# A feed-forward's up projection: every second pair of weight units by seven quarter products

## The reference

```python
def conv_ffn(h, w_up, conv_w, conv_b, w_down):
    u = h @ w_up                                   # 512x1024 by 1024x5632
    ch = u.shape[-1]
    u = lax.conv_general_dilated(u, conv_w, window_strides=(1,), padding=((CONV_W - 1, 0),),
                                 dimension_numbers=('NWC', 'WIO', 'NWC'), feature_group_count=ch) + conv_b
    g, val = jnp.split(u, 2, axis=-1)
    return (jax.nn.gelu(g) * val) @ w_down
```

## Time and profile before

| | |
|---|---|
| three runs | 1375.34, 1376.65, 1377.49 us (median 1376.65) |
| the profiled execution | 1374.93 us, its span 1373.2 us |
| TensorE | 1351.9 us busy, 9440 matmuls |
| VectorE, ScalarE, GpSimd | 743.1, 670.6, 794.4 us busy |
| DMA | 122.81 MB, mean 89 GB/s |
| up projection, from unit 4 on | 435.2 to 652.8 us |

### The profile page before, as it was taken

The page is one execution under the profiler, slowest core; times in us unless marked ns, Lnnn a source line. Parts: engine busy times, 40 slices in busy tenths (PEclk is TensorE's granted clock), DMA queues, the critical chain, the costliest instruction groups (busy, mean ns, idle before and its releaser), DMA issues.

```text
span 1373.2 us, 24197 instructions
## 1 busy us (share of the span) xinstructions
PE 1351.9 (98%) x9440; PEld 1140.9 (83%) x9440; DVE 743.1 (54%) x995; ACT 670.6 (49%) x1172; POOL 794.4 (58%) x599
## 2 busy tenths in 40 slices
PE   9999999999999999999999999999999999999998
PEld 7888787778889888888888887788888878999987
DVE  5135456366556333333554857344379957777732
ACT  4245665364357444444322568566463434445543
POOL 7643342373266666566566447954268856656782
PEclk9999999999999999999999999999999999999999
DMA  6332221221040222222332312200023222233222
GB/s 226 127 119 77 77 77 46 93 106 62 32 169 32 99 101 92 94 105 92 107 107 95 121 50 90 76 19 4 3 79 137 92 93 92 99 102 107 96 104 77
DMA packets 34508, 122.81 MB, mean 89 GB/s; under 512 B 3824, under 2 KB 4336, under 8 KB 34288
## 3 DMA queue, kind: packets, MB, share of 16 engines
q1 hardware_dynamic: 33696, 119.31, 25.5%
q10 hardware_dynamic: 720, 2.20, 0.5%
HBM read 119.40 MB, written 2.10 MB: 88 GB/s over the span
## 4 chain that ended last, share of the span: by engine, by line
PE 91%; issue 3%; DVE 2%; POOL 2%; ACT 2%; ACTq 0%; POOLq 0%; DVEq 0%
PE ps L591 15%; PE ps L593 15%; PE ps L592 15%; PE ps L1427 3%; PE ps L1429 3%; PE ps L1428 3%; PE ps L1358 2%; PE ps L1360 2%; PE ps L1359 2%; PE ps L1495 1%; PE ps L1496 1%; PE ps L1497 1%; POOL w_lo L2231 1%; PE ps L722 1%; PE ps L709 1%
## 5 line engine op out<-in xcount | busy, mean ns | idle before, releaser
L2231 POOL TENSOR_TENSOR w_lo<-stage,w_hi 128x512 fp32r<-128x512 f32 x378 | 556.2, 1496 | 369.1 <-ACT w_hi L1526 364.6
L1526 ACT ACTIVATE w_hi<-stage 128x512 fp32r<-128x512 f32 x376 | 215.4, 623 | 103.2 <-DMA stage<-w 88.0
L591 PE MATMUL ps<-x_hi,w_lo 128*128 128x512 f32 x664 | 262.6, 395 | 0.0
L592 PE MATMUL ps<-x_lo,w_hi 128*128 128x512 f32 x664 | 258.6, 389 | 0.0
L593 PE MATMUL ps<-x_hi,w_hi 128*128 128x512 f32 x664 | 258.6, 389 | 0.0
L591 PEld LDWEIGHTS ps<-x_hi,w_lo 128*128 128x128 f32 x664 | 124.7, 188 | 29.1 <-issue 2.6
L592 PEld LDWEIGHTS ps<-x_lo,w_hi 128*128 128x128 f32 x664 | 124.7, 188 | 26.0 <-issue 1.0
L593 PEld LDWEIGHTS ps<-x_hi,w_hi 128*128 128x128 f32 x664 | 124.6, 188 | 26.1
L2415 POOL TENSOR_TENSOR w_lo<-stage,w_hi 128x512 fp32r<-128x512 f32 x44 | 75.4, 1744 | 53.9 <-DVE s_val L3135 53.9
L2769 DVE SCALAR_TENSOR_TENSOR conv<-ps,vcol,conv 128x511 f32<-128x511 f32 x44 | 33.0, 749 | 132.2 <-ACT conv L1741 132.0
L1741 ACT ACTIVATE conv<-ps,vcol 128x512 f32<-128x512 f32 x44 | 34.3, 779 | 121.1 <-PE ps L593 120.1
(11 more groups left out here) (515 smaller groups left out, 3322.4 us busy)
## 6 DMA issues: line engine op xcount, KB each, us to landing
stage<-w SPq DMA_DIRECT2D x210, 512.0 KB, 3.2
extra_stage<-w SPq DMA_DIRECT2D x6, 512.0 KB, 5.4
H<-xT SPq DMA_DIRECT2D x3, 512.0 KB, 8.6
mem<-memT SPq DMA_DIRECT2D x2, 512.0 KB, 10.6
pool_n<-pool_count ACTq DMA_DIRECT2D x1, 1024.0 KB, 6.1
outT<-outs SPq DMA_DIRECT2D x4, 256.0 KB, 2.0
outT<-outs SPq DMA_DIRECT2D x2, 384.0 KB, 2.7
stage<-w SPq DMA_DIRECT2D x2, 256.0 KB, 3.3
```

The lines of the kernel that those rows point to most:

```text
L591: pe.matmul(out, wl, hi(k), start=first, stop=False)
L592: pe.matmul(out, wh, lo(k), start=False, stop=False)
L1526: act.activation(unit_hi(b)[:, cols], unit_stage(b)[:, cols], ACT.Copy).then_inc(whi_made, 1)
L2231: pool.tensor_tensor(unit_lo(b)[:, cols], unit_stage(b)[:, cols], unit_hi(b)[:, cols].bitcast(F32), ALU.subtract).then_inc(wlo_made, 1)
```

## The change

Eight of the 22 pairs, p = 5, 7, ..., 19, are made by seven quarter products; the other pairs stay whole, in other banks than before where p is even and above 4. The results of a changed pair build up in the rows UX0, UX1, UY0, UY1 of 256 columns in banks 4 to 7, with UE for a product that both columns of the second row get. A running sum is copied by ScalarE from one row to the next (`up_copy`) and TensorE goes on adding on top of the copy; two products of the identity at the start of the stage open the two rows that are never started by a product. `up_add` adds UE at the end, and the taps read two neighbouring rows as one of 512. VectorE's queue gets the weight sums of pair p + 2 (`up_sums`), their low parts and, beside pairs 1 to 3, the four differences of the input. The loops of 12 units are written out. Two DMAs (levels, scan_keep) move from ScalarE's queue after the attention to the end of this stage, because the differences lie where they used to land. The branch stage only counts from other thresholds.

```diff
 UP_BANKS = 4
-UP_TURN = UP_BANKS * AHEAD
+UP_SEVENTHS = tuple(range(5, 20, 2))
...
+        UT_AT = ((24, 28), (80, 84), (A0 + 88, A0 + 92), (A0 + 40, A0 + 84))
+        ut_hi = [at(f"ut_hi{n}", [P, QB, HS], hi, F32R) for n, (hi, lo) in enumerate(UT_AT)]
+        ut_lo = [at(f"ut_lo{n}", [P, QB, HS], lo, F32R) for n, (hi, lo) in enumerate(UT_AT)]
+        ut_val = [at(f"ut_val{n}", [P, QB, HS], lo) for n, (hi, lo) in enumerate(UT_AT)]
+        US_AT = ((101.5, 103.5), (109.5, 111.5), (A0 + 96, 113.5))
+        us_hi = [at(f"us_hi{n}", [P, UNIT // 2], hi, F32R) for n, (hi, lo) in enumerate(US_AT)]
+        us_lo = [at(f"us_lo{n}", [P, UNIT // 2], lo, F32R) for n, (hi, lo) in enumerate(US_AT)]
+        us_val = [at(f"us_val{n}", [P, UNIT // 2], lo) for n, (hi, lo) in enumerate(US_AT)]
...
+        UX0, UX1, UY0, UY1, UE = 9, 10, 13, 14, 15
+        SEVENTHS = len(UP_SEVENTHS)
+        flat = ps[:].rearrange("p b n -> p (b n)")
+        def up_bank(t):
+            p = t // 2
+            return 2 * (p // 2 % 2) + t % 2 if p >= UP_SEVENTHS[0] and p % 2 == 0 else t % UP_BANKS
+        def up_row(t):
+            if t // 2 in UP_SEVENTHS:
+                first = (UX0, UY0)[t % 2] * HS
+                return flat[:, first:first + SEQ]
+            return ps[:, up_bank(t), :]
...
-            with pe.Fori(0, (2 * FFB - UP_BANKS) // UP_TURN) as i:
-                for t in range(UP_BANKS, UP_BANKS + UP_TURN):
-                    up_product(t, i)
-            for t in range(UP_BANKS + (2 * FFB - UP_BANKS) // UP_TURN * UP_TURN, 2 * FFB):
-                up_product(t)
+            def up_seventh(n, wh, wl, hi, lo, start=False):
+                out = quarter[:, n, :]
+                for k in range(QB):
+                    cols = slice(k * P, (k + 1) * P)
+                    pe.matmul(out, wl[:, cols], hi[:, k, :], start=start and k == 0, stop=False, skip_group_check=True)
+                    pe.matmul(out, wh[:, cols], lo[:, k, :], start=False, stop=False, skip_group_check=True)
+                    mm = pe.matmul(out, wh[:, cols], hi[:, k, :], start=False, stop=(k == QB - 1), skip_group_check=True)
+                return mm
+            def up_pair(p):
+                n, b = UP_SEVENTHS.index(p), U0["up"] + 2 * p
+                left, right = slice(0, UNIT // 2), slice(UNIT // 2, UNIT)
+                hi0, lo0, hi1, lo1 = (t[:, (b + d) % RING, :] for d in range(2) for t in (w_hi, w_lo))
+                B11, B21, B22 = ([t[:, QB * r:QB * r + QB, HALF[c]] for t in (x_hi, x_lo)] for r, c in ((0, 0), (1, 0), (1, 1)))
+                T1, T2, T3, T4 = ([ut_hi[j][:], ut_lo[j][:]] for j in range(4))
+                pe.wait_ge(ff_conv, UP_BANKS + 2 * p - 2)
+                pe.wait_ge(wlo_made, 2 * b + 1)
+                up_seventh(UX0, hi0[:, left], lo0[:, left], *B11, start=True).then_inc(st_done_s, 1)
+                if n == 0:
+                    pe.wait_ge(t_lo_s, 4)
+                pe.wait_ge(st_lo_s, 3 * n + 1)
+                up_seventh(UE, us_hi[0][:], us_lo[0][:], *T1, start=True).then_inc(st_done_s, 1)
+                pe.wait_ge(st_lo_s, 3 * n + 2)
+                pe.wait_ge(st_copy_s, 4 * n + 1)
+                up_seventh(UX1, us_hi[1][:], us_lo[1][:], *T2).then_inc(st_done_s, 1)
+                pe.wait_ge(wlo_made, 2 * b + 2)
+                up_seventh(UX0, hi0[:, right], lo0[:, right], *B21)
+                pe.wait_ge(wlo_made, 2 * b + 4)
+                pe.wait_ge(st_copy_s, 4 * n + 3)
+                up_seventh(UY0, hi1[:, left], lo1[:, left], *T3).then_inc(st_done_s, 1)
+                pe.wait_ge(st_lo_s, 3 * n + 3)
+                up_seventh(UX1, us_hi[2][:], us_lo[2][:], *B22).then_inc(unit_done, 1)
+                pe.wait_ge(st_copy_s, 4 * n + 4)
+                up_seventh(UY0, hi1[:, right], lo1[:, right], *T4).then_inc(unit_done, 1)
+            for n in (UX1, UY0):
+                pe.matmul(quarter[:, n, :], ident, con[:, 0:HS], start=True, stop=True)
+            for p in range(UP_HALVES // 2, FFB):
+                if p in UP_SEVENTHS:
+                    up_pair(p)
+                else:
+                    for t in (2 * p, 2 * p + 1):
+                        up_product(t)
...
-            act.dma_start(levels[:], const[:, C0["levels"]:C0["scan"]].rearrange("p (l n) -> p l n", n=HB)).then_inc(levels_in_s, 16)
-            act.dma_start(scan_keep[:], const[:, C0["scan"]:CONST]).then_inc(levels_in_s, 16)
...
+            def up_copy(p, n):
+                i = UP_SEVENTHS.index(p)
+                to, of = ((UX1, UX0), (None, UE), (UY0, UX1), (UY1, UY0))[n]
+                if n == 1:
+                    act.wait_ge(ff_made, p + 1)
+                act.wait_ge(st_done_s, 4 * i + n + 1)
+                act.activation(conv[:, 2 * p % UP_BANKS, 0:HS] if n == 1 else quarter[:, to, :], quarter[:, of, :],
+                               ACT.Copy).then_inc(st_copy_s, 1)
+            def beside_plain(p):
+                if p - 1 in UP_SEVENTHS:
+                    ff_taken(2 * p - 2)
+                    ff_taken(2 * p - 1)
+                up_half_hi(2 * p + 2, 0)
+                up_half_hi(2 * p + 2, 1)
+                up_half_hi(2 * p + 3, 1)
+                if p - 1 in UP_SEVENTHS:
+                    ff_gelu(p - 1)
+                up_sum_hi(p + 1, 0)
+                up_sum_hi(p + 1, 1)
+                act.wait_ge(st_sum_s, 4 * UP_SEVENTHS.index(p + 1) + 2)
+                up_half_hi(2 * p + 3, 0)
+                up_sum_hi(p + 1, 2)
+                ff_taken(2 * p)
+                ff_top(p - 1)
+            def beside_sevenths(p):
+                ff_taken(2 * p - 1)
+                up_half_hi(2 * p + 2, 0)
+                up_copy(p, 0)
+                up_half_hi(2 * p + 2, 1)
+                up_copy(p, 1)
+                ff_gelu(p - 1)
+                up_copy(p, 2)
+                up_half_hi(2 * p + 3, 0)
+                ff_top(p - 1)
+                up_copy(p, 3)
+                up_half_hi(2 * p + 3, 1)
...
+            for p in UP_SEVENTHS:
+                beside_plain(p - 1)
+                beside_sevenths(p)
...
+            act.dma_start(levels[:], const[:, C0["levels"]:C0["scan"]].rearrange("p (l n) -> p l n", n=HB)).then_inc(levels_in_s, 16)
+            act.dma_start(scan_keep[:], const[:, C0["scan"]:CONST]).then_inc(levels_in_s, 16)
...
+            def up_pair_lo(p):
+                b = U0["up"] + 2 * p
+                for n, (d, part, after) in enumerate(((0, 0, 3), (0, 1, 4), (1, 1, 1), (1, 0, 2))):
+                    pool.wait_ge(st_sum_s, 4 * UP_SEVENTHS.index(p) + after)
+                    slot, cols = (b + d) % RING, slice(part * UNIT // 2, (part + 1) * UNIT // 2)
+                    pool.wait_ge(whi_made, 2 * b + n + 1)
+                    pool.tensor_tensor(w_lo[:, slot, cols], stage[:, slot, cols], w_hi[:, slot, cols].bitcast(F32),
+                                       ALU.subtract).then_inc(wlo_made, 1)
+            first_t = 2 * UP_SEVENTHS[0]
+            for t in range(first_t - 3):
                 ff_unit(t)
+            for p in UP_SEVENTHS:
+                up_pair_lo(p)
+                ff_low(p - 2)
+                split_lo(U0["up"] + 2 * p + 2)
+                ff_low(p - 1)
+                split_lo(U0["up"] + 2 * p + 3)
...
+            def up_t(n):
+                if n == 0:
+                    dve.wait_ge(h_made, 2 * KB + BEFORE["h_made"]["xo"])
+                if n >= 2:
+                    dve.wait_ge(t_made_s, n - 1)
+                a, b = ((h_quarter(0, 1), h_quarter(0, 0)), (h_quarter(1, 1), ut_val[0][:]), (h_quarter(1, 1), h_quarter(0, 1)),
+                        (h_quarter(1, 0), ut_val[1][:]))[n]
+                if n == 1:
+                    dve.wait_ge(t_made_s, 1)
+                if n == 3:
+                    dve.wait_ge(t_made_s, 2)
+                dve.tensor_tensor(ut_val[n][:], a, b, ALU.subtract).then_inc(t_made_s, 1)
+            def up_t_low(n):
+                dve.wait_ge(t_hi_s, n + 1)
+                if n < 2:
+                    dve.wait_ge(t_made_s, 4)
+                dve.tensor_tensor(ut_lo[n][:], ut_val[n][:], ut_hi[n][:].bitcast(F32), ALU.subtract).then_inc(t_lo_s, 1)
+            def up_sums(p):
+                n, u = UP_SEVENTHS.index(p), U0["up"] + 2 * p
+                A11, A12, A21, A22 = (stage[:, (u + d) % RING, h * UNIT // 2:(h + 1) * UNIT // 2] for d in range(2) for h in range(2))
+                S1, S2, S4 = (us_val[j][:] for j in range(3))
+                dve.wait_ge(whi_made, 2 * u + 3)
+                if n:
+                    dve.wait_ge(unit_done, u - 2 + CREDIT)
+                dve.tensor_tensor(S1, A21, A22, ALU.add).then_inc(st_sum_s, 1)
+                dve.wait_ge(st_sum_s, 4 * n + 1)
+                dve.tensor_tensor(A21, A11, A21, ALU.subtract).then_inc(st_sum_s, 1)
+                dve.tensor_tensor(S2, S1, A11, ALU.subtract).then_inc(st_sum_s, 1)
+                dve.wait_ge(st_sum_s, 4 * n + 3)
```

(84 more changed lines are left out.)

121 lines of the change are left out of this document (58 added, 63 removed).

## The result

The changed kernel takes 1383.59 us, median of 6 runs (1381.70 to 1385.14), beside 1376.55 for the kernel before on the same chip: ratio 1.0051, 95% interval 1.004 to 1.0061. It is slower by 7.0 us. The forecast was 1380.0, with 1383.5 as the upper end of its range.

A forecast was written before the change was run, and what follows sets the result against it. TensorE's matmul stream was taken to bound the kernel; -6.6 + 0.9 + 6.0 + 1.6 + 1.4 = +3.3 us took the profiled 1374.93 to 1378.2, and the median forecast to 1380.0 us, 8-in-10 range 1371.5 to 1383.5.

The forecast's parts named there:

- What the quarter products save: Eight changed pairs: quarter matmuls spaced 0.1197 us, a pair 10.06 us instead of 10.88, saving 6.6 us in all.
- Rival D: Changed pairs: quarter matmuls run at another spacing, each 5 ns worth 3.4 us, so 1376.6 or 1383.4; chance 0.05.
- The identity matmuls: Ahead of unit 4: two f32 identity products open two banks and add 0.9 us to TensorE.
- The wait for the differences: Pair 5's second quarter product: TensorE waits 6.0 us for VectorE's last low part of a difference.
- rival A: Before pair 5: VectorE's 1024-element operations meet GpSimd less, differences arrive in time, wait 0 to 2 us, 1372.7; chance 0.26.
- Rival B: Before pair 5: half of VectorE's operations find GpSimd idle, wait 3.0 us, clock still lost, 1377.0; chance 0.15.
- The clock behind it: After pair 5's wait: TensorE's clock drops to half for a stretch, costing 1.6 us once.
- The steady pairs: Later changed pairs: all handovers hidden except the fourth copy, which has no reserve; 0.2 x 7 = 1.4 us.
- the third copy: Later changed pairs, ScalarE's copy: due at 26.7 us and ready at 26.2, so no loss.
- Rival C: Seventh product of pairs 7 to 19: fourth copy late each time, 4.2 us instead of 1.4, 1382.8; chance 0.15.
- One sign of being wrong: Whole kernel: the prediction is wrong if the span outside 430 to 660 us changes by more than 1 us.
- the rule that the prediction took from its one case: After every long TensorE wait the clock halves; its case was the 2.96 us wait before 254.98, losing 1.6 us.

The follow-up runs named there:

- Experiment 10: Changed kernel plus early differences, their last two low parts between pair 3's taps, GpSimd's low part of f and ScalarE's fourth copy forward: 1370.99 us, ratio 0.9963.
- experiment 3: Changed kernel with the four differences of the input made earlier, two ahead of pair 0 and two behind pair 1's gating: 1383.79 us, ratio 1.0058.
- experiment 5: Changed kernel with only the last two low parts of the differences moved between pair 3's taps, ahead of the weight sums: 1377.87 us, ratio 1.0006.
- experiment 2: Changed kernel plus 32 unused matmuls of 256 columns ahead of the wait for the differences' low parts: 1382.29 us, ratio 1.0052.
- experiment 6: Changed kernel with GpSimd's low part of f made after the second of four w_lo halves, not after all four: 1382.37 us, ratio 1.0049.
- experiment 8: Changed kernel with both GpSimd's low part of f and ScalarE's fourth copy moved forward: 1377.44 us, ratio 1.0003.
- experiment 7: Changed kernel with ScalarE's fourth copy ahead of the high part of f in each changed pair: 1382.55 us, ratio 1.0038.
- experiment 9: Changed kernel with a changed pair's first weight slot given back after the fourth quarter product instead of the sixth: 1378.72 us, ratio 1.0013.
- experiment 11: Experiment 10 plus the first weight slot of a changed pair given back after the fourth quarter product: 1370.35 us, ratio 0.9965.

## Why the prediction came out wrong

*What the quarter products save: right.* Spacing 0.1197, a pair 10.07 for 10.06. Experiment 10 isolates it: 211.59 - 217.62 - 0.19 = -6.2 where I had -6.6; a whole pair between two quarter ones takes 10.91, not 10.88. Rival D is out.

*The identity matmuls: right*, 0.68 + 0.19 = 0.87 for 0.9.

*The wait for the differences: the place and VectorE right, 4.45 for 6.0, and the reason half wrong.* I followed VectorE's queue and blamed the number and length of the differences. But the sums wait for ScalarE's w_hi, I had even put that at 464.1 (it was 462.5), so what VectorE saves ahead of it is not gained: experiments 3 and 5 show that what mattered was the place of the last two low parts behind the sums. They ended at 474.8 and not at 476.6, nearly all of it from the sums' earlier start. VectorE's operations of 1024 took 2.2 to 2.3 us but for one of 1.21, so rival A's reason is out too. Rival B's 3.0 for this term was as far off as my 6.0.

*The clock behind it: mechanism right (experiment 2), 2.7 for 1.6.* I took the kernel's other stretch as the size, 3.4 us at half clock; this one was 5.9. It isn't fixed: in experiments 6 and 8, behind the same wait, it cost 1.4 to 1.6.

*The steady pairs: the failing step.* "So all is hidden except that the fourth copy has no reserve ... I take 0.2 x 7 = 1.4 us": it was 5.4. The fourth copy, at the seventh product, cost 2.0 of it, not far from the 1.4; the third copy, at the fifth product, which I had put at nothing, cost 3.4. Rival C's 4.2 is nearer in size but names only the seventh product. Three parts of that step failed. The loads were put in as 3.0 to 3.6, read where one is in flight; here two are 1.7 us apart, up to 5.1, and the sums started at 15.9 to 16.6 and not at 14.5 (15.6 to 15.8 in experiment 8, where no pair is late). The third copy I had "due at 26.7 and ready at 26.2" without the waits of the second copy ahead of it in ScalarE's queue, so the path over GpSimd's w_lo and low part of f was missed. And a late copy cost more than its lateness, because the next matmul's spacing was 0.19 to 0.22 where 0.12 is usual. Had these 5.4 us been in the sum, with its other terms as they were, it would have been +7.3, or 1384.0.

The errors of the wait (-1.55) and the clock (+1.1) nearly cancel, the saving adds 0.4 and the pairs 4.0: 3.9 us more than the forecast's +3.3, so 7.2, where the medians have 7.0. That the forecast came within 3.6 us is in part luck, since two errors of over 1 us each had opposite signs. One sign of being wrong that I had named came in the profile, a change of more than 1 us outside the stage (2.0 behind it), but as shown above it is hardly the change's.

## What to carry to other kernels

When TensorE is fed by copies that it waits for within 1.4 us, walk each engine's queue in its issue order and give every instruction its own waits, those of other purposes too: here a low part of f that TensorE reads much later held up the third copy. Where one late chain ends in two places, a cut in its common head helps both, and a cut in one tail may show almost nothing, because the other takes its place. And a long wait of TensorE is to be priced with the clock that it may cost, here 1.4 to 2.8 us behind a wait of 4.2 to 4.4.

## What the runs showed of the hardware

The stretch at 1.2 GHz behind a wait of TensorE was not the same each time. Behind the wait of 4.2 to 4.4 us before pair 5 it cost 2.5 to 2.8 us in the changed kernel and in experiments 3, 7 and 9, and 1.4 to 1.6 in experiments 6 and 8. 32 unused matmuls inside the wait left the clock at 1.00.

The other long wait, 2.96 us before 255, comes in all fourteen profiles and no edit touches it. In twelve the granted clock falls to 0.50 behind it for 3.4 us; in experiments 5 and 11 it does not. Experiment 5, in order of time:

```profile
255.15 0.47 PE L615 MATMUL ps<-o_hi,w_lo 128*128 128x512 f32 x1 [2.96 <-POOL w_lo L2361]
```

and its granted clock:

```profile
256.00:259.00 3.00, 3.00 (x15) 1.00 0.44 172
```

That is why the up stage begins 1.7 us earlier in experiment 5's profile. So the rule that the prediction took from its one case, a loss after every long wait, is not borne out; the measurement decides. And the runs of one kernel differ too: those of the kernel before, beside the experiments, have mean clocks of 0.996 to 1.000 (1380.80 us at 0.996, 1374.03 at 1.000). Why the stretch differs stays open. The Trainium skill (TensorE: Matmul & The Clock Gate, What's actually happening) says that the number of slow matmuls at a start differs from run to run of one kernel; the profiles here agree, for a stretch behind a wait.

The first matmuls after a short handover, of 256 columns, are spaced 0.19 to 0.22 and not 0.12, also where the profile names no wait; seven pairs with two such places lost 5.4 us, and the wait rows name 1.7 of them. In experiment 8, where the copies come in time, the spacing at both places is 0.12.
